# Expert stage of a decoder step: loops over three blocks with three buffers in place of 32 blocks written out, and weight loads issued without a wait for the first rows

## What is computed

```python
eidx, gates = hier_route(h2, r1_w, r1_b, r2_w, r2_b)      # two experts a token, two gates
def expert_block(args):                                   # rows of one expert e
    xb, e = args
    h = jax.nn.silu(xb @ w1[e]) * (xb @ w3[e])            # 1024 -> 512, twice
    return h @ w2[e]                                      # 512 -> 1024
# x + the sum over a token's two experts of gate * expert_block, then a last RMSNorm
```

## Time and profile before

| | |
|---|---|
| median of three runs | 981.95 us |
| profiled execution, its own time | 978.98 us |
| its span in the trace | 977.4 us |
| TensorE busy, weight loads busy | 91%, 60% |
| VectorE, ScalarE, GpSimd busy | 26%, 11%, 16% |
| moved by DMA | 259.36 MB, mean 265 GB/s |
| first and last matmul of the expert stage's blocks | 403.30 us, 941.16 us |

### The profile page before, as it was taken

One profiled execution on the slowest core, in us unless ns is written; L12 is line 12 of the kernel. 1 busy time (PEld: TensorE's weight loads), 2 busy tenths in 40 slices (PEclk: granted clock), 3 DMA queues, 4 the chain that ended last, 5 costly groups with the idle time before them and its releaser, 6 DMA issues. The chain is left out here.

```text
span 977.4 us, 24109 instructions
## 1 busy us (share of the span) xinstructions
PE 891.6 (91%) x10538; PEld 588.6 (60%) x10538; DVE 256.4 (26%) x772; ACT 110.1 (11%) x173; POOL 154.7 (16%) x232
## 2 busy tenths in 40 slices
PE   5999999999999995799999999999999989999940
PEld 2545555454554563677778677866767667686720
DVE  1443454625445356150010101101010101001006
ACT  0210111101011011101001000010101000100104
POOL 1000100000000000211313221322223122131110
PEclk9999999999999998699999999999999999999985
DMA  8770200201021027799999999999999999999838
GB/s 333 280 296 1 87 25 18 86 0 43 0 86 44 3 90 287 304 397 376 368 391 389 402 397 398 390 402 392 408 392 402 395 406 390 404 393 400 340 77 324
DMA packets 57484, 259.36 MB, mean 265 GB/s; under 512 B 10809, under 2 KB 11889, under 8 KB 40356
## 3 DMA queue, kind: packets, MB, share of 16 engines
q1 hardware_dynamic: 47484, 238.51, 61.0%
q0 software_dynamic: 9264, 19.36, 8.0%
q10 hardware_dynamic: 640, 0.07, 0.1%
HBM read 240.86 MB, written 25.04 MB: 272 GB/s over the span
## 5 line engine op out<-in xcount | busy, mean ns | idle before, releaser
L1241 PEld LDWEIGHTS ps<-hT,big 128*64 128x64 f32 x8192 | 292.6, 138 | 45.7 <-issue 44.1
L1241 PE MATMUL ps<-hT,big 128*64 128x80 f32 (+2 forms) x8192 | 300.0, 235 | 19.5 <-issue 17.5
L1264 PE MATMUL ps<-big,poolT 128*80 128x512 f32 (+2 forms) x512 | 191.7, 595 | 1.0 <-issue 0.7
L1138 PE MATMUL ps<-big,hT 128*128 128x512 f32 x384 | 169.5, 601 | 3.6 <-DMA big<-in_w_in 2.3
L1138 PEld LDWEIGHTS ps<-big,hT 128*128 128x128 f32 x384 | 73.1, 192 | 94.7 <-issue 88.4
L1264 PEld LDWEIGHTS ps<-big,poolT 128*80 128x80 f32 (+2 forms) x512 | 64.0, 149 | 104.1 <-issue 101.7
L1033 DVE TENSOR_TENSOR poolT<-u,ps 128x320 f32<-128x320 f32 (+2 forms) x32 | 15.5, 486 | 406.1 <-PE ps L1241 406.1
L552 POOL DMA_INDIRECT x_rows<-xn,sidx x32 | 47.2, 1476 | 363.0 <-ACT xn L732 271.4
L529 POOL DMA_INDIRECT slot_table<-ids,dest x18 | 18.9, 1048 | 303.3 <-DVE dest L849 300.3
L1195 PE MATMUL ps<-big 128*128 128x512 f32 x128 | 56.4, 593 | 0.9 <-DVE big L919 0.9
L1211 PE MATMUL ps<-big 128*128 128x512 f32 x128 | 57.0, 598 | 0.0
(11 more groups left out here) (175 smaller groups left out, 499.6 us busy)
## 6 DMA issues: line engine op xcount, KB each, us to landing
big<-in_exp_w SPq DMA_DIRECT2D x192, 1024.0 KB, 24.4
big<-in_w_in SPq DMA_DIRECT2D x4, 1536.0 KB, 13.3
big<-in_w_out SPq DMA_DIRECT2D x2, 2048.0 KB, 14.9
x_rows<-big SPq DMA_DIRECT2D x8, 512.0 KB, 2.6
h_rows<-xn SPq DMA_DIRECT2D x8, 512.0 KB, 2.9
big<-x_rows SPq DMA_DIRECT2D x8, 512.0 KB, 6.8
out_y_prompt<-big SPq DMA_DIRECT2D x8, 512.0 KB, 2.8
big<-in_x_prompt SPq DMA_DIRECT2D x1, 3072.0 KB, 11.8
```

The source lines that it names most:

```text
L1138: last = pe.matmul(ps[0:m, bank, :], hT[:, k, 0:m], win[:, k, part * AW:(part + 1) * AW], start=(k == 0), stop=(k == KD - 1))
L1241: last = pe.matmul(out[c * w:(c + 1) * w, j, 0:m], up_weights(n)[:, k, j * P + c * w:j * P + (c + 1) * w], xT[:, 4 * half + k, 0:m], start ...
L1264: last = pe.matmul(ps[first:first + m, 5 + cols, :], hhT[:, 2 * half + k, 0:m], down_weights(n)[:, k, cols * 512:(cols + 1) * 512], start= ...
```

## The change

- The stage's blocks go in triples: triple h is the blocks 3h, 3h + 1 and 3h + 2. Triple 0 stands by itself, the triples 1 to 6 (rows 96, 80, 64) are a loop, the triples 7 to 9 (80, 80, 64) a second one, and the blocks 30 and 31 (80, 64) stand written out at the end. Every engine has these loops (`triples`); SP has one loop over the triples 1 to 9.
- What depended on the block's number is now worked out from the loop's counter in a register: semaphore counts, the place in `order`.
- Row buffers, output buffers, indices and gates have three turns instead of two. The third row buffer is `junk`, the third output buffer `bands`, where the constants `band` and `band_prev` have been put together.
- The order of the experts is laid out anew, so that a block finds its expert at the place of its number: `turn_row` holds the ranks in the order of the blocks. Each rank has the same cap as before.
- The wait for the first rows ahead of the weight loads (L450 of before) is gone.
- The waits of TensorE for `y_half_ready` are gone; its later waits cover them.

```diff
-SORTED_CAPS = (96,) * 6 + (80,) * 13 + (64,) * 10
-TURNS = [at for big in range(FIRST // 2) for at in (big, FIRST - 1 - big)] + [FIRST // 2]
-CAPS = [CAP] * SETS + [SORTED_CAPS[at] for at in TURNS]
+CLASSES = ((1, 7, (96, 80, 64)), (7, 10, (80, 80, 64)))
+TURNS = ((1, 7, ((0, 1), (6, 1), (28, -1))), (7, 10, ((12, 2), (13, 2), (22, -1))))
+FINAL, FINAL_CAPS, LEFT = 10, (80, 64), 18
...
-        xg = [sb(f"xg{s}", [P, D]) for s in range(2)]
+        xg = [sb(f"xg{s}", [P, D]) for s in range(2)] + [junk]
...
-        ys = [xn, xn2]
+        ys = [xn, xn2, bands]
...
+        def triples(eng, block_triple):
+
+            block_triple(0, (CAP,) * SETS)
+            for lo, hi, caps_of in CLASSES:
+                with eng.Fori(lo, hi) as h:
+                    block_triple(h, caps_of)
+            block_triple(FINAL, FINAL_CAPS)
...
-            sp.wait_ge(rows_in[0], 16)
+            def load_weights(h, blocks):
+
+                turn = [sp.value_load(order[0:1, bass.ds(h * SETS + (s - SETS), 1)], min_val=0, max_val=NE - 1)
+                        for s in range(blocks)]
+                for n in range(blocks * CH):
+                    s, c = n // CH, n % CH
+                    before = CH * (SETS * h + s - SETS) + c + 1
+                    sp.wait_ge(used, before if isinstance(h, int) else sp.to_reg(before))
+                    load_chunk(turn[s], n)
+
             sp.wait_ge(out_b, NT)
             for n in range(CH, 10):
                 load_chunk(FIRST + 1, n)
...
             sp.wait_ge(order_ready, 1)
-            for b in range(SETS, NE):
-                at = TURNS[b - SETS]
-                turn = sp.value_load(order[0:1, at:at + 1], min_val=0, max_val=NE - 1)
-                for c in range(CH):
-                    sp.wait_ge(used, CH * (b - SETS) + c + 1)
-                    load_chunk(turn, CH * (b % SETS) + c)
+            with sp.Fori(1, FINAL) as h:
+                load_weights(h, SETS)
+            load_weights(FINAL, len(FINAL_CAPS))
...
-            for cap in sorted(set(SORTED_CAPS)):
-                lo, n = SORTED_CAPS.index(cap), SORTED_CAPS.count(cap)
-                pool.memset(caps[:, lo:lo + n], float(NE * cap)).then_inc(caps_set, 1)
+            for lo, hi, caps_of in CLASSES + ((FINAL, FINAL + 1, FINAL_CAPS),):
+                for h in range(lo, hi):
+                    for s, cap in enumerate(caps_of):
+                        at = SETS * (h - 1) + s
+                        pool.memset(caps[:, at:at + 1], float(NE * cap)).then_inc(caps_set, 1)
...
+                    dve.wait_ge(turns_numbered, 1)
+                    for lo, hi, places in TURNS:
+                        for s, (first, by) in enumerate(places):
...
-                 lambda: dve.tensor_scalar(back, beaten, -1.0, float(NE), ALU.mult, ALU.add),
-                 lambda: dve.tensor_scalar(onehot, crow[0:FIRST, NG:NR], back, None, ALU.is_equal)],
+                 lambda: dve.tensor_scalar(onehot, turn_row[0:FIRST, :], beaten, None, ALU.is_equal)],
...
-            for b, m in enumerate(CAPS):
-                run_block(b, m)
+            triples(pe, block_triple)
```

More of the change, by code:

```diff
@@ L70, in reached, with not_first @@
         eng.wait_ge(sem, n)
+def not_first(h, s=0):
+    return not (isinstance(h, int) and h == 0) or s > 0
 def build(nc, x_prompt, x_sample, state_pool, norm1_g, w_in, a_norm_g, a_norm_b, ws_sht, bs_th,
@@ L95, in build @@
         chunk = [big[:, c * CHW:(c + 1) * CHW] for c in range(SETS * CH)]
[L96 to L100, removed]
+        third = 2 * CH * CHW
+        xres = big[:, third:third + NT * D].rearrange("p (j d) -> p j d", d=D)
+        yT = big[:, third + NT * D:third + (NT + 1) * D].rearrange("p (k n) -> p k n", n=P)
+        vg, p, ya, ptail = [big[:, third + (NT + 1) * D + i * AW:third + (NT + 1) * D + (i + 1) * AW] for i in range(4)]
+        done_early = sb("done_early", [P, D + 4 * AW])
         h2T = done_early[:, 0:D].rearrange("p (k n) -> p k n", n=P)
@@ L476, in _ @@
                         sp.dma_start(chunk_dst(c, c), chunk_src(e, c)).then_inc(ov_w, 16)
-            for s in range(2):
-                sp.wait_ge(rows_out[s], 16 * (NE // 2))
+            for s in range(SETS):
+                sp.wait_ge(rows_out[s], 16 * len(range(s, NE, SETS)))
             sp.wait_ge(state_moved, 16)
@@ L612, in _ @@
             pool.wait_ge(order_ready, 1)
-            for b, m in enumerate(CAPS):
-                run_block(b, m)
-            for s in range(2):
-                pool.wait_ge(rows_out[s], 16 * (NE // 2))
+            triples(pool, block_triple)
+            for s in range(SETS):
+                pool.wait_ge(rows_out[s], 16 * len(range(s, NE, SETS)))
             pool.wait_ge(plan_ready, 1)
@@ L942, in _ @@
             take_hT(0, P)
-            dve.wait_ge(filled, 7)
+            dve.wait_ge(filled, 8)
             pipeline(dve, step)
@@ new lines, in block_triple @@
+            def block_triple(h, caps_of):
+                for s, m in enumerate(caps_of):
+                    b = h * SETS + s
+                    pe.wait_ge(xgT_ready, b + 1)
+                    if not_first(h, s):
+                        pe.wait_ge(hhT_ready, b)
+                    for part, out in enumerate((up1, up3)):
+                        for half in range(2):
+                            n = CH * s + 2 * part + half
+                            pe.wait_ge(chunk_in[n], h * 16 + 16)
+                            for k in range(4):
+                                for j in range(KF):
+                                    for c in range(SPLIT):
+                                        w = P // SPLIT
+                                        last = pe.matmul(out[c * w:(c + 1) * w, j, 0:m],
+                                                         up_weights(n)[:, k, j * P + c * w:j * P + (c + 1) * w],
+                                                         xT[:, 4 * half + k, 0:m], start=(half + k + j == 0),
+                                                         stop=(half + k == 4), skip_group_check=True)
+                            last.then_inc(used, 1)
+                            if not not_first(h, s) and part + half == 0:
+                                pe.wait_ge(onehot_ready, 1)
+                                pe.matmul(ps[0:1, 4, 0:NE], key_own[0:FIRST, 0:1], oh[0][0:FIRST, :], start=True,
+                                          stop=True).then_inc(keys_done, 1)
+                    if not isinstance(b, int) or b + 1 < NE:
+                        pe.wait_ge(rows_in[(s + 1) % SETS], h * 16 + (32 if s == SETS - 1 else 16))
+                        turn(xg[(s + 1) % SETS], P, xgT_done)
+                    if not_first(h, s):
+                        pe.wait_ge(y_ready, b)
+                    pe.wait_ge(hhT_ready, b + 1)
+                    for half in range(2):
+                        n = CH * s + 4 + half
+                        pe.wait_ge(chunk_in[n], h * 16 + 16)
+                        for k in range(2):
+                            for cols in range(2):
+                                first = NS * cols if in_halves(m) else 0
+                                last = pe.matmul(ps[first:first + m, 5 + cols, :], hhT[:, 2 * half + k, 0:m],
+                                                 down_weights(n)[:, k, cols * 512:(cols + 1) * 512],
+                                                 start=(half + k == 0), stop=(half + k == 2), skip_group_check=True)
+                        last.then_inc(used, 1)
```

236 lines of the change are left out of this document (109 added, 127 removed).

## The result

| | before | changed |
|---|---|---|
| median of the runs | 982.49 us (980.40 to 984.45, 5 runs) | 988.47 us (986.97 to 990.80, 5 runs) |
| ratio | | 1.0077, 95% interval 1.0049 to 1.0105 |
| profiled execution, its span | 978.98, 977.4 us | 987.98, 986.2 us |

The change made the kernel slower, by 0.8% by the recorded ratio and by 0.6% by the two medians. The forecast was 1006 us: the sign was right, the size four times too large (+24 for +6). Further on the changed kernel turns out to take 988 us on three chips and 978 on one, while the kernel before takes 980 on each of the five chips of the experiments.

A forecast was written before the change was run, and what follows sets the result against it. TensorE was taken to end last, the weight stream 5 us behind. 978.98 + 5.7 (wait) + 19.6 (loops) = 1004.3 us profiled, 1007.3 from the median; forecast 1006 us, range 983 to 1034.

The forecast's parts named there:

- part 4: TensorE's block loops: seven taken branches each refetch the body's start, 6.0 - 3.2 = 2.8 us each, +19.6 us.
- rival 2: Loop body stays in instruction memory; TensorE's pauses, 14 us, go and the weight stream decides: 973 us; chance 0.12.
- Rival 3: At TensorE's loop branches an 8 us fetch leaves a 4.8 us gap and drops the clock: 1040 us; chance 0.13.
- Part 1: Wait for first rows removed: slower slot read and gather start TensorE's stage 7.9 us later; net +5.7 us.
- - 2.2: Last step of Part 1: TensorE's 2.2 us of waiting for weights goes, as the weights lie further ahead.
- Parts 2 and 3: New order of the blocks, and three turns of buffers: taken as 0 us each.
- rival 1: TensorE's loop branches are free, pauses as before, leaving only the removed wait's +5.7: 987.7 us; chance 0.20.

The follow-up runs named there:

- e8: Changed kernel with the wait for the first rows put back and triple 1 written out ahead of the first loop: 991.97 us, ratio 1.0118.
- e4: Changed kernel with two triples in the body of the first loop, about 3360 TensorE instructions: 987.17 us, ratio 1.0058.
- e16: Changed kernel unaltered, on the fifth chip, without dips: 978.34 us, ratio 0.9985.
- e3: Changed kernel, without the wait, with its loops written out, on a chip without dips: 983.63 us, ratio 1.0026.
- e2: Kernel before with only the wait for the first rows taken out, on a chip without dips: 988.33 us, ratio 1.0079.
- e14: Kernel before with only the wait for the first rows taken out, on a chip with dips: 988.64 us, ratio 1.0082.
- e17: Changed kernel with the wait for the first rows put back, on the fifth chip, without dips: 969.82 us, ratio 0.9898.
- e9: Changed kernel unaltered, on a chip with dips: 988.77 us, ratio 1.0090.
- e10: Changed kernel with the wait for the first rows put back, on a chip with dips: 978.58 us, ratio 0.9984.
- e11: Changed kernel, without the wait, with its loops written out, on a chip with dips: 988.01 us, ratio 1.0075.
- e1: Changed kernel with the wait for the first rows put back, on a chip without dips: 969.37 us, ratio 0.9892.
- e7: Changed kernel with the wait put back and triple 7 written out ahead of the second loop, on a chip with dips: 970.0 us, ratio 0.9893.
- e15: Changed kernel with the wait put back and triple 7 written out, on another chip with dips: 972.48 us, ratio 0.9923.
- e18: Changed kernel with the wait put back and triple 7 written out, on the fifth chip, without dips: 967.50 us, ratio 0.9870.

## Why the prediction was wrong

**The step that failed is the count in part 4.** "I expect that the start of the body is no longer there and is fetched again", seven times 2.8 us. The price was right: the branch takes 5.94 us for 6.0, and the gap is 2.78. But it happened once, not seven times. The body stays in the instruction memory, which was the condition of rival 2 (0.12), and its sign came out as stated: 0.67 MB in the instruction queue and the pauses gone from the first loop. The nearest row, the free branch of a short loop, I set aside for its length; the number of the Trainium skill ("Runtime: NRT & Kernel Launch", section "Instruction fetch mechanics"), room for 2048 instructions of TensorE, I set aside for the word FIFO. The runs fit that number as 8 pages of 256: 7 pages touched stay (0.2 us), 8 miss every second time (e8), a body of 3360 misses every time (e4, 6.0 us). They do not fit the rule for a taken branch in the same section of the Trainium skill, which makes it free only within a window of two pages: here branches back over more than six pages took 0.2 us.

**The price of a miss was too small behind the gap.** Besides its 2.78 us there is a second gap a few dozen matmuls on (3.76), and matmuls behind them ran at half the clock (0.50 from 870 to 874 us). In e16, without dips: gaps of 2.82 + 2.83, and 12.78 us for the 256 matmuls that took 9.07 in the earlier trace rows, 9.4 us in all. Rival 3's mechanism was there too, once. In e4's long body a miss has one gap only and costs 4.7 to 5.8 us.

**The gain of the loops was not in the sum.** I compare the stage, from the first matmul of its blocks to the last, in profiles without dips. Written out (e3) it goes from 412.71 to 947.27 us, 534.6 us; with the loops (e16) from 409.87 to 940.41, 530.5 us, of which 9.4 are the missed branch. So the loops gain about 13.4 us of the straight run's pauses. Rival 2 had priced 14 from the idle time of the earlier trace rows.

**Part 1 held, but for its last step.** Forecast: `oidx` 6.0, gather 7.6, start at 411; measured 5.9, 7.1 and 411.30. The DMA engines stood idle until 420 instead of 417.3. What failed is "- 2.2": the waits for weights did not pay any of the delay back; e2 still has 0.8 us of them. (A slip in the same part, 940.8 for 932 + 4.7 + 3.5 = 940.2, changes nothing.) The pairs that differ in the wait alone show +7.9 (e2), +8.5 (e14), +8.5 (e16, e17) and +10.2 (e9, e10) for +5.7.

**Parts 2 and 3, taken as 0.** e3 against e2, on one chip, differ by them alone: 4.7 us faster by the medians. The profiled spans differ by 2.8 us, the stage by 3.1 (537.6 and 534.6), and TensorE's idle time in it by 2.4; which of the two parts it is, and why, stays open. On chips with dips the like pair, e11 and e14, differs by 0.6, but it stands on two chips.

**What no part had: the dips.** They cost the loops 9.2 us (e10 against e1) to 10.4 (e9 against e16), but the kernel with triple 7 written out only 2.5 and 5.0 us (e7 and e15 against e18), in part because e18 waits for weights. The comparison that counted ran on a chip that has them: the 8.8 us block of 64 rows in the changed kernel's profile shows it.

Put together from the profiled spans: 977.4 us before; +8.0 for the start of the stage; -3.3 for parts 2 and 3 (e3's stage for that of before); -13.4 for the pauses; +9.4 for one missed branch; +8.7 for the dips (the stage's 539.3 us for e16's 530.5); -0.6 behind the stage. That gives 986.2, the changed kernel's span. The terms come from several chips, so each is good to a microsecond or two. The step that counts stands out all the same: part 4 had +19.6 for the loops, and they are worth -13.4 + 9.4 = -4.0.

So it was luck that the result lies in the range of the forecast and on rival 1's number, 987.7. Rival 1 had free branches with the pauses left, and neither was so. Even the sign hung on the dips: on chip E the changed kernel came out 1.5 us faster than the kernel before.

## What to carry to other kernels

A loop on TensorE pays if its body, with where it begins, touches no more of the instruction memory's pages than stay there, here 7: then the branch takes 0.2 us and leaves no gap, and the pauses of straight code go. Look at the instruction queue's bytes and at the longest branch, not at the median, to see which case you have. A wait that holds a bulk stream back can be worth more than the stream: here it kept a 0.2 KB read and a gather at 1.9 and 3.8 us on the path, and putting it back gained 8.5 to 10.2 us. With miss and pauses gone, look for the next bound: in e18 it was the stream of weights, as rival 2 had said. And compare kernels on the same chip, on more than one chip.

## What the runs showed of the hardware that I had not expected

- TensorE's instructions come in pages of 256 (16 KB). Straight code of 64-row blocks loses 1.1 to 1.7 us at many of its page borders, that of 80-row blocks mostly 0.3 to 0.9, that of 96-row blocks hardly anything (the kernel before and e3).
- A loop of 1680 instructions over 7 pages: every taken branch about 0.2 us (first loop of the changed kernel, both of e7, the second of e4). Over 8 pages: every second taken branch 5.8 to 7.2 us (second loop of the changed kernel, first of e8). 3360 instructions: both taken ones 6.0 us (e4).
- On three of five chips, and on that of the first comparison, the 256 matmuls of a block of 64 rows, where no page pause stands in it, mostly take 8.6 to 8.9 us instead of 7.7, by stops near matmul 104, 173 and 232, with a granted clock of 1.00 beside them (the window 600 to 700). Blocks of 80 rows take 9.1 to 9.4 us for 9.07, blocks of 96 rows the same 10.73. The stops hit every kernel there at about the same places of a block, looped or not. What causes them was not found.
- What the dips cost depends on the kernel: nothing in the kernel before, 4.4 us in the changed kernel written out, 2.5 and 5.0 with triple 7 alone written out, 9 to 10 with both loops.
